# Delta rule on one Trainium2 core: the transposed inverse from a TensorE transpose and a ScalarE copy, in place of a product and a VectorE subtraction

## The chip, the cores and the metric

The kernel runs on one core of a Trainium2 chip. The metric is the device time of one execution, in microseconds; three executions are shown, and the number that counts is their median. Engines are named as the profile names them: PE is TensorE (PEld its weight loads), DVE is VectorE, ACT is ScalarE, POOL is GpSimd, SP is the engine that issues the DMAs.

## The reference

The kernel computes one step of a two-layer backbone over 1024 sample tokens and 256 context tokens. The change touches one part of layer 0, the gated delta rule, which runs in two directions over the tokens with four heads of 128 channels. For each chunk of tokens the reference does

```
decay = jnp.where(tri_incl, jnp.exp(jnp.where(tri_incl, diff, 0.0)), 0.0)
lmat = jnp.where(tri_strict, jnp.einsum('bnhik,bnhjk->bnhij', kb, kc) * decay, 0.0)
amat = lmat + jnp.eye(C, dtype=q.dtype)
sol = lax.linalg.triangular_solve(amat, rhs, left_side=True, lower=True, unit_diagonal=True)
...
def step(s, xs):
    v_new = u_i - jnp.einsum('bhck,bhkv->bhcv', w_i, s)
    o = jnp.einsum('bhck,bhkv->bhcv', qd_i, s) + jnp.einsum('bhij,bhjv->bhiv', qk_i, v_new)
    s = s * cd_i[..., None, None] + jnp.einsum('bhck,bhcv->bhkv', kd_i, v_new)
```

What matters here is the solve with a unit triangular matrix; everything is fp32.

## The kernel before

The program is a list of stages that are written out one behind the other for each engine, with semaphores between the engines. The stage in question is the delta rule in `mixer_even`. It takes the 1280 tokens in chunks of 128 (`IT` is 10 of them) and inverts the 128x128 unit triangular matrix of each head and chunk by doubling. There are seven levels (`LEVELS`). Level 0 gives an inverse of 2x2 blocks, levels 1 to 6 (`LV`) join two blocks of the inverse to one of twice the size. The kernel holds the inverse twice: `Y`, and its transpose `X`. Four heads of 128 columns lie in one bank of 512, so a product of "four heads" is four matmuls of 128x128 in fp32, which the trace shows as eight instructions, and a transpose of four heads is four instructions.

Level `v` consists of two stages, `r` and `u`:

- In stage `r` GpSimd masks the triangular matrix for this level (`lm`, line 1319, into one of two buffers), TensorE multiplies mask and Y (`r`, line 1169, bank 0), and ScalarE copies the product to SBUF as `R` (line 1290).
- In stage `u` TensorE forms R<sup>T</sup>X (`q`, line 1173, bank 1; not at level 6, where nobody needs X any more), and X<sup>T</sup>R (`u`, line 1174, bank 2). VectorE subtracts the first from X (`x`) and the second from Y (`y`), both through the helper at line 1203. The next level's `r` waits for `y`.

Ahead of the levels stand the stages start, decay, rates, exps, scores, mask and inverse, which make the decay factors, the triangular matrix and the first X and Y (X transposed at line 1161, copied at line 1287). Behind them stand state, new and out: KS (line 1180), two VectorE steps, the new values (line 1183, copied by ScalarE at line 1293), the outputs (lines 1189 and 1190) and the state's update (line 1192).

The order is written out by hand: `SCHEDULE` steps through the 22 stages of a chunk for the forward direction (`d` 0) and, `LAG` = 3 stages behind it, the backward direction (`d` 1), and every engine follows that one list. So in the levels TensorE's queue reads: r of forward level k, q and u of backward level k-2, q and u of forward level k, r of backward level k-1, r of forward level k+1. Each direction has four banks of PSUM and buffers of its own. Within the first chunk the list also carries four pieces of pooling work, at the forward stages u1 to u4: an ACT copy (line 1053) and a POOL subtraction (line 1057) each.

Of the kernel before, what the change touches and what calls it, by code (L numbers as in the profile page):

```python
# [41 lines left out]
LEVELS = 7  # L42
# [117 lines left out]
def build(nc, A, OUT):  # L160
    with ExitStack() as ctx:
# [515 lines left out]
        def mixer_even(before_norm, prev, h_ready, early):  # L677
# [399 lines left out]
                ring_out.load(eng, i, w_out[:, :, m * P:(m + 1) * P], (KD, P))  # L1077
            pn = ["gb", "gc", "kk", "qk", "kt", "vt", "xt"]
            for v in LV:
                pn += [f"r{v}"] + ([f"q{v}"] if v < LEVELS - 1 else []) + [f"u{v}"]  # L1080
            pn += ["ks", "vn", "o", "ds"]
            vn = ["gu", "gc", "ta", "tb", "tc", "gl", "l", "qk", "nb", "kd", "vb", "x"]
            for v in LV:
                vn += ([f"x{v}"] if v < LEVELS - 1 else []) + [f"y{v}"]
            vn += ["r1", "r2", "o", "s1", "s2"]
            pe_d = [steps(f"pe_dn{d}", pn, IT) for d in "fb"]
            ve_d = [steps(f"ve_dn{d}", vn, IT) for d in "fb"]
            ac_d = [steps(f"ac_dn{d}", ["eb", "ea", "cd", "eq", "eg", "egl", "y"] + [f"r{v}" for v in LV] + ["vn"], IT) for d in "fb"]
            po_d = [steps(f"po_dn{d}", ["lb", "lm0", "qd"] + [f"lm{v}" for v in LV], IT) for d in "fb"]
            s_state, s_new = sem("state_landed"), sem("state_stored")  # L1090
            s_zb = sem("z_back")
# [41 lines left out]
            @program("pe")  # L1133
            def _(eng):
                ended(eng, *part1, *part2)
                eng.wait_ge(s_small, 64)

                def heads(d, b, f):
                    for hd in range(HEADS):
                        m = f(bank(d, b)[:, hd, :], hd)  # L1140
                    return m
                for stage, d, it in SCHEDULE:
                    pe, ve, ac, po, bf, cs = pe_d[d], ve_d[d], ac_d[d], po_d[d], B[d], cols(it, d)
                    v = int(stage[1:]) if stage[1:].isdigit() else 0
                    if stage == "decay":
                        eng.wait_ge(ve.sem, ve.at("gu", it))
                        if it:
                            eng.wait_ge(ac.sem, ac.at("vn", it - 1))
                        eng.matmul(PS[:, 4 * d, :], ones, bf["R"].rearrange("p h t -> p (h t)"), start=True, stop=True).then_inc(*pe.did("gb", it))
                        eng.matmul(PS[:, 4 * d + 3, 0:4], SQM[:, d, :], GG[:, chunk(it, d), 4 * d:4 * d + 4], start=True, stop=True).then_inc(*pe.did("gc", it))  # L1150
                        heads(d, 1, lambda o, hd: eng.matmul(o, KT[:, hd, cs], KT[:, hd, cs], start=True, stop=True)).then_inc(*pe.did("kk", it))
                        heads(d, 2, lambda o, hd: eng.matmul(o, KT[:, hd, cs], QT[:, hd, cs], start=True, stop=True)).then_inc(*pe.did("qk", it))
                    elif stage == "scores":
                        eng.wait_ge(ve.sem, ve.at("gc", it))
                        heads(d, 3, lambda o, hd: eng.transpose(o, KT[:, hd, cs], ident)).then_inc(*pe.did("kt", it))
                        eng.wait_ge(ve.sem, ve.at("gl", it))
                        eng.wait_ge(ac.sem, ac.at("eq", it))
                        heads(d, 0, lambda o, hd: eng.transpose(o, VT[:, hd, cs], ident)).then_inc(*pe.did("vt", it))
                    elif stage == "inverse":
                        eng.wait_ge(ve.sem, ve.at("x", it))  # L1160
                        heads(d, 3, lambda o, hd: eng.transpose(o, bf["X"][:, hd, :], ident)).then_inc(*pe.did("xt", it))
                    elif v and stage[0] == "r":
                        if v == 1:
                            eng.wait_ge(ac.sem, ac.at("y", it))
                        else:
                            eng.wait_ge(ve.sem, ve.at(f"y{v - 1}", it))
                        eng.wait_ge(po.sem, po.at(f"lm{v}", it))
                        lm = bf[f"M{v % 2}"]
                        heads(d, 0, lambda o, hd: eng.matmul(o, lm[:, hd, :], bf["Y"][:, hd, :], start=True, stop=True)).then_inc(*pe.did(f"r{v}", it))  # L1169
                    elif v:  # L1170
                        eng.wait_ge(ac.sem, ac.at(f"r{v}", it))
                        if v < LEVELS - 1:
                            heads(d, 1, lambda o, hd: eng.matmul(o, bf["R"][:, hd, :], bf["X"][:, hd, :], start=True, stop=True)).then_inc(*pe.did(f"q{v}", it))  # L1173
                        heads(d, 2, lambda o, hd: eng.matmul(o, bf["X"][:, hd, :], bf["R"][:, hd, :], start=True, stop=True)).then_inc(*pe.did(f"u{v}", it))  # L1174
                    elif stage == "state":
                        if it:
                            eng.wait_ge(ve.sem, ve.at("s2", it - 1))
                        else:
                            eng.wait_ge(s_state, 32)
                        heads(d, 3, lambda o, hd: eng.matmul(o, KT[:, hd, cs], bf["S"][:, hd, :], start=True, stop=True)).then_inc(*pe.did("ks", it))  # L1180
                    elif stage == "new":
                        eng.wait_ge(ve.sem, ve.at("r2", it))
                        heads(d, 0, lambda o, hd: eng.matmul(o, bf["Y"][:, hd, :], bf["R"][:, hd, :], start=True, stop=True)).then_inc(*pe.did("vn", it))
                    elif stage == "out":
                        eng.wait_ge(ac.sem, ac.at("vn", it))
                        eng.wait_ge(po.sem, po.at("qd", it))

                        def out(o, hd):
                            eng.matmul(o, bf["S"][:, hd, :], bf["QD"][:, hd, :], start=True, stop=False)  # L1189
                            return eng.matmul(o, bf["VN"][:, hd, :], bf["QK"][:, hd, :], start=False, stop=True)  # L1190
                        heads(d, 1, out).then_inc(*pe.did("o", it))
                        heads(d, 2, lambda o, hd: eng.matmul(o, bf["KD"][:, hd, :], bf["VN"][:, hd, :], start=True, stop=True)).then_inc(*pe.did("ds", it))

            @program("ve")
            def _(eng):
                ended(eng, *part1, *part2)
                eng.wait_ge(s_small, 64)
                for stage, d, it in SCHEDULE:
# [31 lines left out]
                    elif v and stage[0] == "u":  # L1230
# [3 lines left out]
                            eng.wait_ge(ac.sem, ac.at("y", it))  # L1234
                        else:
                            eng.wait_ge(ve.sem, ve.at(f"y{v - 1}", it))
                        if v < LEVELS - 1:
                            tt(f"x{v}", bf["X"], bf["X"], bank(d, 1), ALU.subtract)
                        tt(f"y{v}", bf["Y"], bf["Y"], bank(d, 2), ALU.subtract)
                    elif stage == "state":  # L1240
                        eng.wait_ge(pe.sem, pe.at("ks", it))
# [25 lines left out]
            @program("ac")  # L1267
            def _(eng):
                ended(eng, *part1, *part2)
                for stage, d, it in SCHEDULE:  # L1270
                    pe, ve, ac, bf, cc = pe_d[d], ve_d[d], ac_d[d], B[d], C[d]
                    v = int(stage[1:]) if stage[1:].isdigit() else 0
                    if (d, it) == (0, 0) and stage in POOL_AT_STAGE:
                        pool_hi(eng, POOL_AT_STAGE.index(stage))
                    if (stage, d, it) == ("start", 0, NS // P):
                        ring_out.hi(eng, 0)
                    if stage == "exps":
                        eng.wait_ge(ve.sem, ve.at("gl", it))
                        eng.activation(bf["QK"], bf["QK"], ACT.Exp).then_inc(*ac.did("eb", it))
                        eng.activation(bf["L"], bf["L"], ACT.Exp, scale=-1.0).then_inc(*ac.did("ea", it))  # L1280
                        eng.activation(cc["cd"], bank(d, 0)[:, :, LAST[d]], ACT.Exp).then_inc(*ac.did("cd", it))
                        eng.activation(bf["QD"], bank(d, 0), ACT.Exp).then_inc(*ac.did("eq", it))
                        eng.activation(cc["eg"], cc["gc"], ACT.Exp).then_inc(*ac.did("eg", it))
                        eng.activation(cc["egl"], cc["gl"], ACT.Exp).then_inc(*ac.did("egl", it))
                    elif stage == "inverse":
                        eng.wait_ge(pe.sem, pe.at("xt", it))
                        eng.activation(bf["Y"], bank(d, 3), ACT.Copy).then_inc(*ac.did("y", it))
                    elif v and stage[0] == "r":
                        eng.wait_ge(pe.sem, pe.at(f"r{v}", it))
                        eng.activation(bf["R"], bank(d, 0), ACT.Copy).then_inc(*ac.did(f"r{v}", it))  # L1290
                    elif stage == "new":
                        eng.wait_ge(pe.sem, pe.at("vn", it))
                        eng.activation(bf["VN"], bank(d, 0), ACT.Copy).then_inc(*ac.did("vn", it))
# [1371 lines left out]
```

## Time and profile before

| | |
|---|---|
| median of 3 runs | 4584.02 us (4581.57 to 4584.15) |
| the profiled execution | 4592.9 us, of which its span 4591.1 us |
| busy over the whole span | PE 89%, PEld 75%, DVE 52%, ACT 22%, POOL 25% |
| mean granted TensorE clock | 0.947 |

Times in the trace count from the start of the span. A line of the timeline gives start, length, engine, line of the code, operation, what it writes and reads, how many instructions are merged into it, and in brackets how long the engine was idle before it and who released it. Weight loads (PEld) run ahead of their matmuls; the distance between the starts of two PEld groups is what a group takes of TensorE's time. The clock column is the share of full clock that TensorE was granted: 1.00 is 2.4 GHz and 0.50 is 1.2 GHz.

### The profile page before, as it was taken

To read this page: it belongs to the slowest core of one execution; us is meant where nothing else is said; L and a number is where in the kernel's file an instruction comes from. 1 tells how busy PE (TensorE), PEld (TensorE's weight loads), DVE (VectorE), ACT (ScalarE), POOL (GpSimd) and SP (SyncE) were. 2 spreads that over 40 slices of the span, in tenths; PEclk is the share of its full clock that TensorE was granted. 3 is DMA by queue.
4 is the path that set the end of the run, shared out by engine and by line. 5 is a ranking of instruction groups with operands and counts; after the bars stand their busy time and mean duration, and the time that the engine had idled before them with its cause. 6 is when DMAs were issued, how large, how long until landed. Compare 5 with 4: busy or idle time off the path is not lost.

```text
span 4591.1 us, 52229 instructions
## 1 busy us (share of the span) xinstructions
PE 4094.1 (89%) x22424; PEld 3442.3 (75%) x22424; DVE 2404.3 (52%) x2654; ACT 1031.2 (22%) x1460; POOL 1156.0 (25%) x579
## 2 busy tenths in 40 slices
PE   5899788778989999999969999987667899999998
PEld 3687677777768888888747777776556688888886
DVE  4373445554235444434457556679982445444443
ACT  3153221221131111111233343211111311111112
POOL 1111334333242222222331000022221422222224
PEclk7999999999889999999979999988888899999998
DMA  6511000000212122122122222241321011111111
GB/s 240 164 35 32 29 1 1 1 19 3 85 42 60 56 66 64 59 60 60 42 95 66 85 96 79 72 157 67 122 94 37 23 42 36 36 37 37 41 37 68
DMA packets 309550, 280.99 MB, mean 61 GB/s; under 512 B 8885, under 2 KB 285830, under 8 KB 305831
## 3 DMA queue, kind: packets, MB, share of 16 engines
q1 hardware_dynamic: 309320, 277.65, 18.4%
q8 instruction: 178, 2.92, 0.3%
q14 instruction: 52, 0.43, 0.0%
HBM read 219.94 MB, written 57.67 MB: 60 GB/s over the span
## 4 chain that ended last, share of the span: by engine, by line
PE 64%; DVE 17%; issue 3%; ACT 2%; POOL 2%; DMA 1%; SPq 0%; POOLq 0%; DVEq 0%; ACTq 0%
PE PS L670 47%; DVE piece L1783 8%; PE PS L1851 5%; DVE piece L1203 3%; PE PS L1173 2%; PE PS L1174 2%; PE PS L1169 2%; PE PS L2024 1%; DVE piece L2192 1%; DVE piece L1719 1%; PE PS L1624 1%; ACT piece L510 1%; DVE piece L2220 1%; DVE piece L2195 0%; PE PS L1189 0%
## 5 line engine op out<-in xcount | busy, mean ns | idle before, releaser
L670 PE MATMUL PS<-piece,piece 128*128 128x512 f32 (+1 forms) x13896 | 2810.1, 362 | 79.8 <-POOL piece L545 36.8
L670 PEld LDWEIGHTS PS<-piece,piece 128*128 128x128 f32 x13896 | 2322.5, 191 | 539.5 <-issue 107.0
L653 POOL TENSOR_TENSOR piece<-piece,piece 128x1024 fp32r<-128x1024 f32 (+1 forms) x205 | 507.7, 2477 | 2581.9 <-ACT piece L647 2581.9
L1851 PE MATMUL PS<-piece,piece 128*128 128x256 f32 x1920 | 441.6, 392 | 128.1 <-DVE piece L2478 111.4
L1719 DVE SCALAR_TENSOR_TENSOR piece<-piece,piece,piece 128x1024 f32<-128x1024 f32 x352 | 534.8, 1519 | 12.6
L1851 PEld LDWEIGHTS PS<-piece,piece 128*128 128x128 f32 x1920 | 376.7, 197 | 188.2 <-DVE piece L2478 114.2
L1739 DVE SCALAR_TENSOR_TENSOR piece<-PS,piece,piece 128x1024 f32<-128x1024 f32 x224 | 187.8, 880 | 417.2 <-PE PS L670 417.2
L647 ACT ACTIVATE piece<-piece 128x1024 fp32r<-128x1024 f32 (+1 forms) x205 | 206.4, 1007 | 662.5 <-PE PS L670 615.4
L1203 DVE TENSOR_TENSOR piece<-piece,PS 128x512 f32<-128x512 f32 x288 | 185.4, 684 | 265.3 <-PE PS L1174 206.8
L1716 DVE TENSOR_SCALAR piece<-piece,piece 128x1024 f32<-128x1024 f32 x44 | 35.8, 813 | 514.5 <-ACT piece L1666 514.5
L1169 PE MATMUL PS<-piece,piece 128*128 128x128 f32 x960 | 142.6, 295 | 57.1 <-DVE piece L1203 39.5
L1669 ACT ACTIVATE piece<-piece 128x1280 f32<-128x1280 f32 x44 | 56.1, 1274 | 607.5 <-DVE piece L1727 607.5
L1319 POOL TENSOR_TENSOR piece<-piece,piece 128x512 f32<-128x512 f32 x120 | 159.7, 1345 | 116.0 <-PE PS L1169 116.0
L1783 DVE TENSOR_TENSOR piece<-piece 128x512 f32<-128x512 f32 (+2 forms) x168 | 179.0, 1066 | 17.9 <-ACT piece L2443 11.7
L1169 PEld LDWEIGHTS PS<-piece,piece 128*128 128x128 f32 x960 | 123.4, 201 | 72.9 <-DVE piece L1203 51.9
L1783 DVE SCALAR_TENSOR_TENSOR piece<-piece 128x512 f32<-128x512 f32 (+1 forms) x288 | 163.0, 566 | 9.9
L2192 DVE TENSOR_TENSOR piece<-piece,PS 128x512 f32<-128x512 f32 x80 | 52.9, 684 | 176.9 <-PE PS L2024 176.9
L2457 POOL TENSOR_TENSOR piece<-piece,piece 128x512 f32<-128x512 f32 x40 | 57.5, 1438 | 340.6 <-DVE piece L2478 340.6
L1290 ACT ACTIVATE piece<-PS 128x512 f32<-128x512 f32 x120 | 71.7, 597 | 289.1 <-PE PS L1169 289.1
L1665 ACT ACTIVATE piece<-PS 128x1024 f32<-128x1024 f32 x44 | 45.3, 1029 | 401.4 <-PE PS L670 401.4
L1685 POOL TENSOR_TENSOR piece<-piece,piece 128x1280 fp32r<-128x1280 f32 x44 | 129.9, 2952 | 1.9 <-ACT piece L1673 1.5
L1174 PE MATMUL PS<-piece,piece 128*128 128x128 f32 x960 | 128.3, 280 | 0.0
(238 smaller groups left out, 3505.3 us busy)
## 6 DMA issues: line engine op xcount, KB each, us to landing
piece<-in_l_ffn_up SPq DMA_DIRECT2D x88, 512.0 KB, 3.7
piece<-in_l_w_in SPq DMA_DIRECT2D x45, 512.0 KB, 3.7
piece<-in_l_ada_w SPq DMA_DIRECT2D x44, 512.0 KB, 5.2
piece<-in_l_ada_w SPq DMA_DIRECT2D x18, 1024.0 KB, 7.9
piece<-in_l_ffn_down SPq DMA_DIRECT2D x48, 384.0 KB, 3.0
piece<-filters_s SPq DMA_DIRECT2D x8, 2176.0 KB, 9.6
filters_s<-piece SPq DMA_DIRECT2D x64, 256.0 KB, 2.0
hyena_tokens<-piece SPq DMA_DIRECT2D x24, 640.0 KB, 4.0
```

The source lines that it names most:

```text
L647: eng.activation(HI[i % 2][0][:, 0:n], RAW[i % raws][:, 0:n], ACT.Copy).then_inc(*self.ac.did("hi", i))
L653: eng.tensor_tensor(LO[i % 2][0][:, 0:n], RAW[i % raws][:, 0:n], HI[i % 2][1][:, 0:n], ALU.subtract)\
L670: m = eng.matmul(PS[:, bank + b, 0:n], w, x[:, a:a + n], start=first and n_ == 0, stop=last and n_ == 2)
L1169: heads(d, 0, lambda o, hd: eng.matmul(o, lm[:, hd, :], bf["Y"][:, hd, :], start=True, stop=True)).then_inc(*pe.did(f"r{v}", it))
L1174: heads(d, 2, lambda o, hd: eng.matmul(o, bf["X"][:, hd, :], bf["R"][:, hd, :], start=True, stop=True)).then_inc(*pe.did(f"u{v}", it))
L1203: eng.tensor_tensor(out, a, b, op).then_inc(*ve.did(step, it))
L1319: eng.tensor_tensor(bf[f"M{v % 2}"], bf["L"], over(LVM[:, d, v, :], HEADS), ALU.mult).then_inc(*po.did(f"lm{v}", it))
L1685: eng.tensor_tensor(hl, CV[j % 2], hh, ALU.subtract).then_inc(*po.did("lo", j))
L1719: eng.scalar_tensor_tensor(acc, src, w, acc, ALU.mult, ALU.add).then_inc(*ve.did(f"grid{k}", j))
L1739: eng.scalar_tensor_tensor(XT[:, mm, a:a + n], PSF[:, at_:at_ + n], MOD[:, layer, 40 + mm, c:c + 1], XT[:, mm, a:a + n], ALU.mult, ALU.add ...
L1783: f(*args).then_inc(*st.did(f"{tag}{n[0]}", rnd))
L1851: m = eng.matmul(PS[:, bank, o * HC:(o + 1) * HC], M[i][o], rhs[i], start=i == 0, stop=i == 1)
```

## The change

At levels 2 to 6 X is no longer updated by a product and a subtraction. Once Y of the level before is there, TensorE transposes it into bank 1 (`t`, right behind `r` in its queue), and ScalarE copies that bank to X (`x`, right behind the copy of R in its queue). Stage u waits for this copy, which stands behind that of R. At level 1 X is still what the stage before the levels left, so there is neither a product nor a transpose. Level 6, which had no update of X, now has a transpose and a copy like the others.

```
-                pn += [f"r{v}"] + ([f"q{v}"] if v < LEVELS - 1 else []) + [f"u{v}"]
+                pn += [f"r{v}"] + ([f"t{v}"] if v > 1 else []) + [f"u{v}"]
...
                         heads(d, 0, lambda o, hd: eng.matmul(o, lm[:, hd, :], bf["Y"][:, hd, :], start=True, stop=True)).then_inc(*pe.did(f"r{v}", it))
+                        if v > 1:
+                            heads(d, 1, lambda o, hd: eng.transpose(o, bf["Y"][:, hd, :], ident)).then_inc(*pe.did(f"t{v}", it))
...
-                        eng.wait_ge(ac.sem, ac.at(f"r{v}", it))
-                        if v < LEVELS - 1:
-                            heads(d, 1, lambda o, hd: eng.matmul(o, bf["R"][:, hd, :], bf["X"][:, hd, :], start=True, stop=True)).then_inc(*pe.did(f"q{v}", it))
+                        eng.wait_ge(ac.sem, ac.at(f"r{v}" if v == 1 else f"x{v}", it))
                         heads(d, 2, lambda o, hd: eng.matmul(o, bf["X"][:, hd, :], bf["R"][:, hd, :], start=True, stop=True)).then_inc(*pe.did(f"u{v}", it))
...
-                        if v < LEVELS - 1:
-                            tt(f"x{v}", bf["X"], bf["X"], bank(d, 1), ALU.subtract)
                         tt(f"y{v}", bf["Y"], bf["Y"], bank(d, 2), ALU.subtract)
...
                         eng.activation(bf["R"], bank(d, 0), ACT.Copy).then_inc(*ac.did(f"r{v}", it))
+                        if v > 1:
+                            eng.wait_ge(pe.sem, pe.at(f"t{v}", it))
+                            eng.activation(bf["X"], bank(d, 1), ACT.Copy).then_inc(*ac.did(f"x{v}", it))
```

## Rows read from the trace of the kernel before

**Rows 1.** the page's chain that ended last, share of the span by line

```profile
PE PS L670 47%; DVE piece L1783 8%; PE PS L1851 5%; DVE piece L1203 3%; PE PS L1173 2%; PE PS L1174 2%; PE PS L1169 2%; PE PS L2024 1%; DVE piece L2192 1%; DVE piece L1719 1%; PE PS L1624 1%; ACT piece L510 1%; DVE piece L2220 1%; DVE piece L2195 0%; PE PS L1189 0%
```

**Rows 2.** groups of instructions, 473 to 1152 us: count, busy us, mean ns, idle before

```profile
L1203 DVE TENSOR_TENSOR piece<-piece,PS 128x512 f32<-128x512 f32 x288 | 185.4, 684 | 265.3 <-PE PS L1174 206.8 <-PE PS L1192 43.8 <-ACT piece L1280 14.1
L1319 POOL TENSOR_TENSOR piece<-piece,piece 128x512 f32<-128x512 f32 x120 | 159.7, 1345 | 116.0 <-PE PS L1169 116.0
L1169 PE MATMUL PS<-piece,piece 128*128 128x128 f32 x960 | 142.6, 295 | 57.1 <-DVE piece L1203 39.5 <-POOL piece L1319 10.6 <-ACT piece L1287 6.9
...
L1173 PE MATMUL PS<-piece,piece 128*128 128x128 f32 x800 | 112.8, 287 | 0.0
...
L1057 POOL TENSOR_TENSOR piece<-piece,piece 128x1280 fp32r<-128x1280 f32 x4 | 11.6, 2895 | 11.2 <-ACT piece L1053 11.2
```

**Rows 3.** the timeline, one level of both directions: start us, us, engine, line

```profile
906.63 1.16 PE L1169 MATMUL PS<-piece,piece 128*128 128x128 f32 x8 [0.48 <-DVE piece L1203]
...
907.83 0.60 ACT L1290 ACTIVATE piece<-PS 128x512 f32<-128x512 f32 x1 [1.04 <-PE PS L1169]
...
908.41 0.97 PEld L1174 LDWEIGHTS PS<-piece,piece 128*128 128x128 f32 x8
...
909.30 0.97 PEld L1173 LDWEIGHTS PS<-piece,piece 128*128 128x128 f32 x8
...
909.61 1.28 DVE L1203 TENSOR_TENSOR piece<-piece,PS 128x512 f32<-128x512 f32 x2 [3.04 <-PE PS L1174]
...
911.09 0.97 PEld L1169 LDWEIGHTS PS<-piece,piece 128*128 128x128 f32 x8
...
911.40 1.28 DVE L1203 TENSOR_TENSOR piece<-piece,PS 128x512 f32<-128x512 f32 x2 [0.50 <-PE PS L1174]
...
912.74 1.16 PE L1169 MATMUL PS<-piece,piece 128*128 128x128 f32 x8 [0.48 <-DVE piece L1203]
```

**Rows 4.** the timeline, two groups of four transposes, one behind the other

```profile
949.08 0.47 PEld L1155 LDWEIGHTS PS<-piece,piece 128*128 128x128 f32 x4
...
949.52 0.47 PEld L1158 LDWEIGHTS PS<-piece,piece 128*128 128x128 f32 x4
```

**Rows 5.** the timeline of GpSimd, the mask of level 2

```profile
898.44 1.27 POOL L1319 TENSOR_TENSOR piece<-piece,piece 128x512 f32<-128x512 f32 x1
```

**Rows 6.** the timeline, level 2's and level 6's first product and the end

```profile
900.06 1.16 PE L1169 MATMUL PS<-piece,piece 128*128 128x128 f32 x8 [1.38 <-DVE piece L1203]
...
924.96 1.16 PE L1169 MATMUL PS<-piece,piece 128*128 128x128 f32 x8 [0.48 <-DVE piece L1203]
...
935.44 0.30 PEld L1189 LDWEIGHTS PS<-piece,piece 128*128 128x128 f32 x2
...
938.12 0.97 PEld L1174 LDWEIGHTS PS<-piece,piece 128*128 128x128 f32 x8
```

**Rows 7.** the timeline of ScalarE, Y of the forward direction in four chunks

```profile
892.50 0.60 ACT L1287 ACTIVATE piece<-PS 128x512 f32<-128x512 f32 x1 [9.46 <-PE PS L1161]
...
957.58 0.60 ACT L1287 ACTIVATE piece<-PS 128x512 f32<-128x512 f32 x1 [9.45 <-PE PS L1161]
...
1023.90 0.60 ACT L1287 ACTIVATE piece<-PS 128x512 f32<-128x512 f32 x1 [9.28 <-PE PS L1161]
...
1091.06 0.60 ACT L1287 ACTIVATE piece<-PS 128x512 f32<-128x512 f32 x1 [9.46 <-PE PS L1161]
```

**Rows 8.** the chain in order of time, at half clock: transposes, and a product

```profile
895.23 0.85 PE PS L1155 x4
...
968.65 1.71 PE PS L1173 x8
```

**Rows 9.** the last transposes: timeline, then clock in stretches of them (PE, PEld, PEclk)

```profile
4574.70 9.11 PE L2563 MATMUL PS<-piece,piece 128*128 128x128 f32 x56 [1.40 <-DVE piece L2575]
...
4574.70:4578.70 4.00, 4.00 (x19) 4.00 (x20) 0.50 0.45 178
...
4579.70:4583.80 4.10, 3.97 (x34) 3.41 (x32) 1.00 0.95 385
```

More of the change, by code:

```diff
@@ L1083, in mixer_even @@
             for v in LV:
-                vn += ([f"x{v}"] if v < LEVELS - 1 else []) + [f"y{v}"]
+                vn += [f"y{v}"]
             vn += ["r1", "r2", "o", "s1", "s2"]
@@ L1087, in mixer_even @@
             ve_d = [steps(f"ve_dn{d}", vn, IT) for d in "fb"]
-            ac_d = [steps(f"ac_dn{d}", ["eb", "ea", "cd", "eq", "eg", "egl", "y"] + [f"r{v}" for v in LV] + ["vn"], IT) for d in "fb"]
+            ac_d = [steps(f"ac_dn{d}", ["eb", "ea", "cd", "eq", "eg", "egl", "y"] + [f"{t}{v}" for v in LV for t in "rx" if t == "r" or v > 1] + ["vn"], IT) for d in "fb"]
             po_d = [steps(f"po_dn{d}", ["lb", "lm0", "qd"] + [f"lm{v}" for v in LV], IT) for d in "fb"]
```

## The prediction

> **What bounds the kernel now.** I read the page's chain first, for the share of the span that the change can touch. The big products at line 670 hold 47% of it; the delta rule appears as VectorE's line 1203 with 3% and TensorE's lines 1173, 1174 and 1169 with 2% each [rows 1]. It is a serial stage on the path that ends last, so what it saves comes off the total. The groups of instructions in that stage come next. Line 1173, the product that the change takes out, has 800 instructions, 100 groups of eight; line 1169 waited for VectorE 39.5 us, for GpSimd 10.6 us and for ScalarE 6.9 us [rows 2]. TensorE and VectorE alternate here, and GpSimd's masks are late only rarely.
>
> The timeline then shows one level of both directions (F forward, B backward). F's r starts at 906.63, its next one at 912.74 [rows 3]: 6.11 us. A group of four heads takes 0.89 us of TensorE (908.41 to 909.30). In its queue stand r of F, q and u of B, q and u of F, r of B: six groups, 5.34 us, and a gap of 0.77. The loop closes through F alone: F's u ends at 911.09, VectorE starts 0.31 us later, needs 1.28 us for x and y, and r starts 0.06 us after that [rows 3]. Two things thus set the period: six groups, and a VectorE turn that only B's r covers in part.
>
> **Part 1: q goes, t comes.** 100 products of 0.89 us leave TensorE. 100 transposes of four heads come; two such groups stand back to back at 949.08 and 949.52 [rows 4], so 0.44 us each. TensorE saves 45 us of work. These are fp32 transposes of four 128x128 tiles as well, so the row is the price and needs no bounds.
>
> **Part 2: VectorE's x goes.** Each turn shrinks from 1.28 to 0.68 us [rows 2, 3].
>
> **Part 3: ScalarE's copy comes, and u waits for it.** The copy of R starts 1.20 us after r's first instruction and lasts 0.60 (907.83 against 906.63) [rows 3]. The transposes end 1.33 us after r's start and could be copied from 1.64, 0.31 later, so R is last, not t. The copy of X comes behind R: from 1.80 to 2.40, and u may start at 2.46 with the hand-over of 0.06. For the copy I take 0.60, the same shape out of the same kind of bank. From below, a copy that overlapped R's until the transposes allow it would end at 2.24; from above, twice a copy, 1.20, would end it at 3.00. Behind the waiting u on TensorE stands r of the other direction; behind the waiting copy on ScalarE stands the other direction's copy of R. Both are in the sums below. No DMA is issued, and SP waits for nothing new.
>
> **Part 4: the new period.** Count from F's r. r to 0.89, t to 1.33, u of B to 2.22 (its X was copied in the half-turn before), wait to 2.46, u of F to 3.35, r of B to 4.24, t of B to 4.68. F's y: 3.35 plus 0.31 plus 0.68 plus 0.06 is 4.40, so F's next r starts at 4.68. B's y is ready at 3.27, before r of B is wanted at 3.35. TensorE now sets the period but for a wait of 0.24: 4.68 in place of 6.11, 1.43 less.
>
> **Part 5: one interval** (F's and B's chunk side by side).
> - Level 1 to 2: the first u comes 0.89 earlier and VectorE's turn is shorter, which would put F's r of level 2 at about 898.6. The mask of level 2 ends at 899.71 [rows 5]; the r starts then in place of 900.06 [rows 6]. Saved 0.33, and GpSimd is what is late next.
> - Level 2 to 3: before, 6.57 us (900.06 to 906.63). After: R from 1.20, X copied to 2.40, u from 2.46 to 3.35, y and hand-over 1.05: 4.40. Saved 2.17. The transpose of B's first X in between is 1.2 us earlier too, since VectorE comes to it earlier by the first x and the first q.
> - Levels 3 to 6: three periods, 4.29.
> - From F's r of level 6 (924.96) to B's u of level 6 (938.12) [rows 6]: 13.16 us before. After: eight groups (r, u, r, KS, u, new values, r of B, u of B's level 5 among them) 7.12, three transposes 1.32, the outputs 2.68 (935.44 to 938.12 [rows 6]), and the waits: 0.24 for each of two X copies, and 0.62 for VectorE's two steps behind KS, so far covered by B's q and u. Sum 12.22, saved 0.94. Here level 6 pays for a transpose and a copy that it did not have.
>
> The sum is 7.7 us. What follows, from state to the next chunk's first Y, has neither step and shifts as it is.
>
> **Part 6: ten intervals.** The four starts of Y shown lie 65.08, 66.32 and 67.16 us apart [rows 7]; of the eight regular intervals five have 65.08. The longer ones have the half clock in a bad place: a group of products costs 1.71 and of transposes 0.85 there [rows 8]. The first interval is another case: four GpSimd pieces of 2.9 us, each waiting for a ScalarE copy that follows a copy of R [rows 2], make masks late (the 10.6 us). The new X copy stands ahead of three of them and adds some 0.6 us each, which takes nearly all that its last levels gain: I count zero. Nine times 7.7 is **69 us**.
>
> The profiled execution (4592.9 us) would become 4524; it is 8.9 us above the median of 4584.02. On the median the sum gives 4515 us.
>
> **Rivals.**
> 1. *The half clock falls among the levels.* The stretch at half clock, about one per interval, lies now mostly beside work that other engines bound; with another interval length it may land in levels that TensorE itself sets. The three long intervals paid 1.2 to 2.1 us for it. At 2 us in each of nine: 18 us given back, 4533. For it: TensorE has little slack left in the new period. Against: five of eight pay nothing.
> 2. *The X copy is slow to be handed over.* If it takes the upper bound, u starts at 3.06 and the period is 5.28: 0.60 lost in each of six turns per interval, 32 us over nine, 4547. The copies of R in the trace speak against it: 0.60 each [rows 3].
> 3. *The masks become the bound, no gain.* GpSimd needs two masks a period, 2.7 us at their mean of 1345 ns [rows 2]; it would need 3.05 each to hold the period at 6.11. 4584 then; only the first interval looks like that.
> 4. *Slower: transposes let the clock fall.* If TensorE ran at half clock through the levels, the period would be four groups of 1.71 and two transposes of 0.85, 8.54 in place of 6.11: 7.3 us lost over three periods. The end would take 8 x 1.71 + 3 x 0.85 + 2 x 2.68 = 21.6 in place of 13.2, 8.4 lost, and level 2 about 1. That is 17 us an interval, 150 over nine: 4734 us. It decides from the point where a third of the levels' time runs so: 7.7 gained against 24.4 (17 and 7.7) lost. Against it stand the kernel's last 56 transposes, a TensorE stretch of nothing else: it began at 0.50 and reached 1.00, which it held from 4579.70 on [rows 9]. The Trainium skill, in "TensorE: Matmul & The Clock Gate", section "Part 4: PE-mode transpose", says that transposes don't count as busy and leave the clock at its lower level; by it this rival would be the likely one. The trace disagrees with the rule in that stretch, so I give it little.
>
> **How the numbers follow.** The forecast, 4515, gets 0.78; rival 1, 0.10; rival 2, 0.06; rival 3, 0.02; rival 4, 0.04. The range starts at 4500: with the lower bound of the copy TensorE's 4.44 us sets the period, a further 0.24 less in each of six turns, about 9.1 us saved per interval, 82; the rest of the way to 4500 is the excess of the long intervals, if it goes. It ends at 4547 with the slow copy, and so holds about nine in ten. A measurement of this kernel tells some 0.2% (9 us) from no change: faster 0.94, same 0.02, slower 0.04.
>
> **What would show it.** In the changed trace F's r of one level should follow that of the level before by 4.6 to 4.7 us; line 1173 should be gone and 400 instructions of transposes be there at 0.44 a group; ScalarE should copy twice back to back, the second ending 2.4 us after r's start; VectorE should have one subtraction a turn; intervals should be near 57.4 us, the first near 78. I am wrong if the X copy ends later than 3.0, if GpSimd releases r within the levels of later chunks, or if the clock column shows 0.50 through levels 3 to 6.

## The result, and the profile after

The changed kernel takes 4520.4 us (median of 4 runs, 4517.9 to 4522.6) against 4584.09 us (4581.57 to 4587.15) beside it: ratio 0.9854 [0.9843, 0.9865], 63.7 us saved. The forecast was 4515, its range 4500 to 4547.

The profiled execution (4520.36 us, span 4518.5 us) has this chain that ended last, from the page:

```profile
PE PS L670 47%; DVE piece L1784 8%; PE PS L1852 5%; PE PS L1169 2%; DVE piece L1203 2%; PE PS L1174 2%; PE PS L2025 1%; PE PS L1171 1%; DMA piece<-hyena_tokens 1%; DVE piece L2193 1%; DVE piece L1720 1%; POOL piece L1311 1%; PE PS L1625 1%;
```

Beside [rows 1], VectorE's line 1203 has 2% in place of 3%; the product of line 1173 (2%) is gone and the transposes, now line 1171, have 1%. The groups of instructions of the delta rule, 473 to 1090 us, answer to [rows 2] (the masks are line 1320 now, the R copy 1288, the X copy 1291):

```profile
L1320 POOL TENSOR_TENSOR piece<-piece,piece 128x512 f32<-128x512 f32 x120 | 158.0, 1337 | 56.3 <-PE PS L1169 55.9
L1169 PE MATMUL PS<-piece,piece 128*128 128x128 f32 x960 | 142.5, 297 | 43.2 <-POOL piece L1320 36.3 <-ACT piece L1285 6.9
...
L1203 DVE TENSOR_TENSOR piece<-piece,PS 128x512 f32<-128x512 f32 x188 | 126.5, 686 | 250.8 <-PE PS L1174 189.7 <-PE PS L1192 46.3 <-ACT piece L1278 14.1
...
L1171 PE MATMUL PS<-piece,piece 128*128 128x128 f32 x400 | 64.2, 286 | 0.0
L1291 ACT ACTIVATE piece<-PS 128x512 f32<-128x512 f32 x100 | 59.2, 592 | 2.3 <-PE PS L1171 2.3
```

Three things are to be seen. The 288 subtractions are 188. Line 1169 no longer waits for VectorE (39.5 us before) but for GpSimd's masks: 36.3 us where 10.6 stood, 18.2 of it in the first interval and 18.2 behind it. And the X copies waited 2.3 us in all for the transposes, so they stand right behind the R copies. One level of both directions, from the timeline (columns as in [rows 3]):

```profile
755.93 0.97 PEld L1169 LDWEIGHTS PS<-piece,piece 128*128 128x128 f32 x8
...
756.82 0.47 PEld L1171 LDWEIGHTS PS<-piece,piece 128*128 128x128 f32 x4
...
757.13 0.60 ACT L1288 ACTIVATE piece<-PS 128x512 f32<-128x512 f32 x1 [0.24 <-PE PS L1169]
757.26 1.98 PEld L1174 LDWEIGHTS PS<-piece,piece 128*128 128x128 f32 x16
...
757.63 0.59 ACT L1291 ACTIVATE piece<-PS 128x512 f32<-128x512 f32 x1
758.46 0.69 DVE L1203 TENSOR_TENSOR piece<-piece,PS 128x512 f32<-128x512 f32 x1 [2.91 <-PE PS L1174]
759.21 0.97 PEld L1169 LDWEIGHTS PS<-piece,piece 128*128 128x128 f32 x8
...
760.53 0.97 PEld L1169 LDWEIGHTS PS<-piece,piece 128*128 128x128 f32 x8
```

F's r comes again after 4.60 us (6.11 before). The R copy starts 1.20 after r, as before; the X copy starts 0.50 behind it, not 0.60, and ends at 758.22, 2.29 after r's start. The u of B and of F are merged into one block of 16 there. Cut at 758.24, the timeline of TensorE's loads shows where the eight loads of F's u begin:

```profile
758.27 0.97 PEld L1174 LDWEIGHTS PS<-piece,piece 128*128 128x128 f32 x8
```

The u of B begins at 757.26 and takes 0.89, so TensorE could go on at 758.15. F's u waits 0.12 more and begins 0.05 behind the end of the X copy (758.22). It ends at 759.16, and r of B begins at 759.21, 0.06 behind the end of B's subtraction (758.46 and 0.69). The same two small waits stand in all 36 such blocks behind the first chunk. The chain in order of time (start, us, what) holds nothing but TensorE there:

```profile
756.20 0.89 PE PS L1169 x8
757.10 0.44 PE PS L1171 x4
757.53 1.90 PE PS L1174 x16
759.43 0.94 PE PS L1169 x8
760.37 0.44 PE PS L1171 x4
760.80 0.89 PE PS L1169 x8
```

0.89 + 0.44 + 1.90 + 0.94 + 0.44 is 4.61: TensorE's queue is the whole period. Its work is 4.44 of that (four groups of 0.89, two of 0.44); the rest is the two waits, which the chain counts into u (1.90) and r (0.94). What closes the loop is u of B (0.89), B's subtraction with its hand-overs (1.05), then r and t of B and r and t of F (2.66): 4.60. The u of F runs beside that subtraction, and its wait for the X copy is nearly covered by it.

**Where the 63.7 us came from.** The unchanged kernel was run again with a profile (below: "before again"), because the profile of before was a long execution, and the changed one too ("after again"). The intervals between the first X transposes of F (line 1161) in consecutive chunks, the last one up to the store of the final state, in us:

| | first | the eight regular ones | last |
|---|---|---|---|
| before | 77.84 | 66.66, five of 65.08, 66.32, 67.15 | 61.82 |
| before again | 77.72 | 66.70, five of 65.07 or 65.08, 64.71, 65.08 | 61.93 |
| after | 79.93 | three of 57.01, five of 57.82 to 58.19 | 52.23 |
| after again | 81.97 | 56.99 and 57.00, six of 57.87 to 58.29 | 52.23 |

Against "before again" the stage shrank by 67.7 us (661.50 to 593.77): 60.2 in the regular intervals and 9.7 in the last, less 2.2 that the first one lost. Between before and "after again" it shrank by 68.1 (665.19 to 597.09). What lies behind the stage took 3436.3 us in "before again" and 3437.8 in after; over all fourteen profiles it lies between 3432.6 and 3443.2, though no edit touches it.

### The profile page after: what moved, and what is told of

Same layout as the page of the kernel before. It is cut to its first block, busy times and chain, and to the rows that moved or that the text cites. A ratio compares the mean times of both kernels' runs of the same rounds, so it can differ in the third digit from the quotient of the medians.

```text
span 4518.5 us, 51429 instructions
## 1 busy us (share of the span) xinstructions
PE 4047.1 (90%) x22024; PEld 3400.1 (75%) x22024; DVE 2342.4 (52%) x2554; ACT 1080.9 (24%) x1560; POOL 1155.1 (26%) x579
## 4 chain that ended last, share of the span: by engine, by line
PE 64%; DVE 16%; POOL 3%; issue 2%; ACT 2%; DMA 2%; SPq 0%; POOLq 0%; DVEq 0%; ACTq 0%
PE PS L670 47%; DVE piece L1784 8%; PE PS L1852 5%; PE PS L1169 2%; DVE piece L1203 2%; PE PS L1174 2%; PE PS L2025 1%; PE PS L1171 1%; DMA piece<-hyena_tokens 1%; DVE piece L2193 1%; DVE piece L1720 1%; POOL piece L1311 1%; PE PS L1625 1%; DVE piece L2221 1%; ACT piece L510 0%
## 5 line engine op out<-in xcount | busy, mean ns | idle before, releaser
L1203 DVE TENSOR_TENSOR piece<-piece,PS 128x512 f32<-128x512 f32 x188 | 126.5, 686 | 250.8 <-PE PS L1174 189.7
L1169 PE MATMUL PS<-piece,piece 128*128 128x128 f32 x960 | 142.5, 297 | 43.2 <-POOL piece L1320 36.3
L2193 DVE TENSOR_TENSOR piece<-piece,PS 128x512 f32<-128x512 f32 x80 | 52.8, 684 | 175.3 <-PE PS L2025 175.3
L2444 ACT ACTIVATE piece<-PS 128x512 f32<-128x512 f32 x80 | 47.8, 597 | 350.0 <-PE PS L1852 350.0
```

The lines of the kernel that those rows point to most:

```text
L1203: eng.tensor_tensor(out, a, b, op).then_inc(*ve.did(step, it))
```

## The experiments

Each kernel was timed against the unchanged kernel on the same chip. "Period" is F's r to F's next r within the levels; "stage" runs from the first X transpose to the store of the final state.

**Both kernels again.** No edit.

> The kernel before once more, with a profile of its own. Its profiled execution had been 4592.9 us and its runs 4581.6 to 4587.2, so the changed kernel gained 72 us in the traces and 64 us in the medians. Theory A (the stretches at half clock fall differently in each execution): the regular intervals are 65.08 us again where no half clock falls among the levels, the delta rule ends up to 8 us earlier, and the rest of the span is the same to 1 or 2 us. Theory B (the difference lies elsewhere in the kernel): the delta rule takes 677 us again and the rest differs.

Measured: 4585.9 us, ratio 1.0002 [0.9993, 1.0011]. Its profiled execution took 4580.36 us, where that of before took 4592.9; the first X transpose stands at 480.79 against 486.99, and the stage took 661.50 against 665.19. So 6.2 us of before's excess lay ahead of the stage, where the change touches nothing, 3.7 in it and 2.6 behind it. Neither theory had that: the half clock within the stage can account for the 3.7 at most.

> The changed kernel once more, with a profile of its own. Theory A: its regular intervals are 57.0 us where no half clock falls among the levels and about 58.2 where one does, the first 79.9; the ratio to the kernel before is 0.985 again (0.984 to 0.987).

Measured: 4520.0 us, 0.9852 [0.9832, 0.9872]. The regular intervals are as expected, 57.0 twice and 57.87 to 58.29 six times; the first is not: 81.97 in place of 79.9.

**What all of X costs.** The transposes and the X copy go, and u waits for R alone.

```diff
-                        if v > 1:
-                            heads(d, 1, lambda o, hd: eng.transpose(o, bf["Y"][:, hd, :], ident)).then_inc(*pe.did(f"t{v}", it))
...
-                        eng.wait_ge(ac.sem, ac.at(f"r{v}" if v == 1 else f"x{v}", it))
+                        eng.wait_ge(ac.sem, ac.at(f"r{v}", it))
...
-                            eng.activation(bf["X"], bank(d, 1), ACT.Copy).then_inc(*ac.did(f"x{v}", it))
```

> Levels 2 to 6 keep the X of level 0: no transposes, no copies of X. Part of the computation is left out. Theory A (the chain r, copy of R, copy of X, u, y sets the period, with TensorE close behind): the period falls from 4.60 to 3.80 us, an interval from 57.0 to 52.9, the kernel from 4520 to about 4480 us. Theory B (TensorE's work alone decides and the copy is hidden): 0.44 us less for each of 100 transposes, 44 us spread over two directions, the period falls by 0.88 to 3.7 and the time to 4476; the two differ here by little, and the next run separates them.

Measured: 4480.6 us, 0.9775 [0.976, 0.9789]; period 3.78, as Theory A had it (3.80, where B had 3.7), stage 556.2; the times of the two theories lie too near to be told apart. So, with all else as it is, 39.8 us is the most that a still faster way to X could give: the change took 63.7 of 103.5.

**The X copy twice.** ScalarE copies the bank once more, ahead of the real copy, into a buffer that is free then.

```diff
+                            eng.activation(bf["VN"], bank(d, 1), ACT.Copy).then_inc(*ac.did(f"w{v}", it))
                             eng.activation(bf["X"], bank(d, 1), ACT.Copy).then_inc(*ac.did(f"x{v}", it))
```

> ScalarE copies the transposed bank twice, first to a buffer that nobody reads, then to X. Theory A (the copy stands on the chain): 0.5 us more per turn, the period 5.1, an interval 60, the kernel 4520 plus 29, 4549 us. Theory B (the copy is hidden beside TensorE's work): no change, 4520.

Measured: 4543.4 us, 0.9918 [0.9902, 0.9935]. The chain in order of time over one period:

```profile
762.78 0.60 ACT piece L1288
763.38 0.49 ACT piece L1291
763.87 0.49 ACT piece L1292
764.36 0.49 ACT piece L1288
764.85 0.49 ACT piece L1291
765.34 0.50 ACT piece L1292
765.83 0.04 issue
765.88 1.16 PE PS L1174 x8
767.04 0.91 PE PS L1169 x8
767.94 0.02 issue
767.97 0.60 ACT piece L1288
```

The period is 5.19, and it closes through ScalarE: six copies of 0.49 to 0.60, then u and r. Take the two extra copies (0.98) out and the same loop is 4.21, below the 4.60 of TensorE. So in the changed kernel ScalarE's queue has 0.4 us a period to spare, and does not set the period; the X copy holds up only u of F, by the 0.12 that B's subtraction nearly covers. The expectation came out in size (period 5.1, 4549 us), the mechanism as the rows tell it: it is ScalarE's whole queue that counts, not the one late copy.

**The X copy on VectorE.**

```diff
-                            eng.activation(bf["X"], bank(d, 1), ACT.Copy).then_inc(*ac.did(f"x{v}", it))
...
+                        eng.tensor_copy(bf["X"], bank(d, 1)).then_inc(*ve.did(f"x{v}", it))
```

> VectorE copies the transposed bank to X, in place of ScalarE, at the same stage. Theory A: VectorE has room there (the copy would run from 1.64 to 2.32 us after r starts, the other direction's y from 2.53), so the period stays near 4.60 and the kernel at 4520, at most 2 us less in the first interval; that ScalarE does it is not where the gain comes from. Rival (VectorE's turn was the bound, and any second operation on it costs its 0.6 us again): 0.6 us per turn, 60 us over 100 turns less what overlaps, 4560 to 4580.

Measured: 4517.4 us, 0.9855 [0.984, 0.9869]; period 4.66, with two VectorE operations a turn as in the kernel before (6.11). That it is ScalarE that copies gives nothing: what helps is that the subtraction no longer stands behind u on the path.

**The transpose as a product with the identity.** Same bank, same order, but eight instructions of a product in place of four of a transpose.

```diff
-                            heads(d, 1, lambda o, hd: eng.transpose(o, bf["Y"][:, hd, :], ident)).then_inc(*pe.did(f"t{v}", it))
+                            heads(d, 1, lambda o, hd: eng.matmul(o, bf["Y"][:, hd, :], ident, start=True, stop=True)).then_inc(*pe.did(f"t{v}", it))
```

> Each transpose is replaced by a product of Y with the unit matrix, which gives the same X at a product's price (0.89 us for four heads in place of 0.44). Theory A (TensorE's six groups and the chain set the period): the period rises from 4.60 to about 5.4, an interval from 57.0 to 61.3, the kernel to about 4559 us; most of what the change gains over the period of 6.11 then remains with the removed VectorE step and the order. Rival (transposes let the clock fall, products hold it): the clock column shows fewer stretches at 0.50 than in the changed kernel, and the time comes out below 4545.

Measured: 4564.6 us, 0.9957 [0.994, 0.9974]. One period, from the table of stretches (PE busy, PEld, DVE, ACT, POOL, clock, DMA share, GB/s):

```profile
843.72:849.24 5.52, 5.52 (x51) 5.50 (x50) 1.38 (x2) 2.39 (x4) 1.28 (x2) 1.00 0.01 3
```

The period rises by 0.92, about twice the 0.45 by which a product exceeds a transpose, since TensorE is busy throughout. Of the 63.7 us, 44.2 hang on the transpose being half as long as a product; the other 19.5 are what is gained even at a product's price, with the subtraction off the path and a copy beside TensorE's work in its place. One sign of the rival did appear: over the eight regular intervals the granted clock is 0.98, where the changed kernel had 0.96 (0.95 in "after again"). Its time, below 4545, did not. And the transposes are not what sets that clock: over the same intervals it is 0.95 in the run without any in the levels ("What all of X costs"), and 0.98 in the next run, which has all of them.

**Transposes ahead of r.** t and the X copy go ahead of r and the R copy; u waits for R.

```diff
+                        if v > 1:
+                            heads(d, 1, lambda o, hd: eng.transpose(o, bf["Y"][:, hd, :], ident)).then_inc(*pe.did(f"t{v}", it))
                         eng.wait_ge(po.sem, po.at(f"lm{v}", it))
...
                         heads(d, 0, lambda o, hd: eng.matmul(o, lm[:, hd, :], bf["Y"][:, hd, :], start=True, stop=True)).then_inc(*pe.did(f"r{v}", it))
-                        if v > 1:
-                            heads(d, 1, lambda o, hd: eng.transpose(o, bf["Y"][:, hd, :], ident)).then_inc(*pe.did(f"t{v}", it))
```

> The transposes stand ahead of r in TensorE's queue and the copy of X ahead of that of R. Theory A: u then waits for the copy of R, 2.30 us after the turn's start, the period is 4.5 in place of 4.6; at level 2 the transposes run while r waits for its mask, 0.44 less. About 0.9 us per interval, 8 us in all, and 2 us in the first interval: 4510 us. Rival (the copy of X hides behind TensorE anyway): 4520, no change.

Measured: 4499.5 us, 0.9813 [0.9799, 0.9828], 20.9 us under the changed kernel, where Theory A had 10. The period fell little, 4.60 to 4.55; regular intervals went from 57.01 to 56.43. The timeline at F's level 2 shows one place:

```profile
739.14 0.42 PEld L1168 LDWEIGHTS PS<-piece,piece 128*128 128x128 f32 x4 [0.97 <-DVE piece L1203]
...
740.40 0.97 PEld L1171 LDWEIGHTS PS<-piece,piece 128*128 128x128 f32 x8 [0.83 <-POOL piece L1320]
```

The transposes now run while r still waits for the mask. Seven of eight regular intervals lie at 56.43 to 56.59, so the long ones are nearly gone, and the last interval took 48.8. The stage shrank by 13.2 (593.8 to 580.5); the remaining 7.7 of the 20.9 us lie outside it in the two profiles, where the edit does nothing. Behind the stage it is 5.2 (3437.8 to 3432.6), and there the clock records of the traces hold 342 us at half clock in after and 327 here; why the half clock falls less often there stays open.

**Masks one level early.** GpSimd makes the mask of level v+1 at stage r of level v, so that no r waits for it.

```diff
-                        eng.tensor_tensor(bf[f"M{v % 2}"], bf["L"], over(LVM[:, d, v, :], HEADS), ALU.mult).then_inc(*po.did(f"lm{v}", it))
+                        for lv in ((1, 2) if v == 1 else (v + 1,) if v + 1 < LEVELS else ()):
...
+                            eng.tensor_tensor(bf[f"M{lv % 2}"], bf["L"], over(LVM[:, d, lv, :], HEADS), ALU.mult).then_inc(*po.did(f"lm{lv}", it))
```

> GpSimd makes each mask from level 2 on one stage earlier, in time that it spends waiting. Theory A (at level 2 the mask is what is late next, and in the first interval the masks are late behind the pooling pieces): about 1.2 us less in each of nine intervals, 8 us in the first, 4501 us; no idle time of line 1169 put down to GpSimd after the first interval. Rival (at level 2 the next thing, VectorE's x of the other direction, is late at once): 4515 to 4520.

Measured: 4506.6 us, 0.9829 [0.9815, 0.9844], between the two theories; but the gain is the first interval's alone (79.93 to 66.77), and no regular one is under 57.52, where after has three of 57.01. F's r of level 2 did start 1.94 behind u of level 1 rather than 3.25, and line 1169 waited for GpSimd 7.8 us in place of 36.3. But 7.8 us of waiting for VectorE came instead, and u of level 1 itself stands 1.09 later in its interval. The timeline of after, one interval's beginning (GpSimd and VectorE):

```profile
738.42 1.72 POOL L1320 TENSOR_TENSOR piece<-piece,piece 128x512 f32<-128x512 f32 x1
...
739.85 1.45 DVE L1203 TENSOR_TENSOR piece<-piece,piece 128x512 f32<-128x512 f32 x2
```

and the same place with the early masks, with the ScalarE step that waits:

```profile
838.77 3.41 POOL L1321 TENSOR_TENSOR piece<-piece,piece 128x512 f32<-128x512 f32 x2
...
840.20 2.52 DVE L1203 TENSOR_TENSOR piece<-piece,piece 128x512 f32<-128x512 f32 x2
...
842.83 0.63 ACT L1277 ACTIVATE piece<-piece 128x512 f32<-128x512 f32 x1 [2.12 <-DVE piece L1203]
```

The second mask of GpSimd runs beside two VectorE operations that read both inputs from SBUF: they take 2.52 in place of 1.45, and B's exponentials, which were idle 1.04 there, wait 2.12. That is the 1.07 us that B's whole chunk starts later. B's first r then comes 0.84 later, and F's r of level 3, behind it in TensorE's queue, 0.68.

**The pooling pieces ahead of the chunks.** The four GpSimd pieces move from the levels u1 to u4 of the first chunk to its early stages.

```diff
-            POOL_AT_STAGE = ["u1", "u2", "u3", "u4"]
+            POOL_AT_STAGE = ["start", "decay", "rates", "exps"]
```

> The four pooling pieces (a copy on ScalarE and a subtraction on GpSimd each) move from the first chunk's stages u1 to u4 to its stages start to exps. Theory A (they make the first interval 79.9 us in place of 57.0, since GpSimd's masks stand behind them and each waits for a copy that now follows the copy of X): the first interval falls to about 63 us, with the first masks 5 us later, the kernel to 4503. Rival (the first interval is long for other reasons, cold queues or the half clock): 4515 to 4520.

Measured: 4507.5 us, 0.9829 [0.9813, 0.9846]. The first interval is 58.03, like any other (63 expected), but it starts at 497.33, 10.4 later than in after (5 expected): the four pieces stand ahead of the first masks, and behind the DMA that brings the masks' constants. From the timeline of GpSimd:

```profile
481.75 11.43 POOL L1057 TENSOR_TENSOR piece<-piece,piece 128x1280 fp32r<-128x1280 f32 x4 [31.39 <-DMA piece<-in_k_level]
```

**Both, and the pieces split.** Transposes first, two pieces at the start and two behind the levels.

```diff
-            POOL_AT_STAGE = ["u1", "u2", "u3", "u4"]
+            POOL_AT_STAGE = ["start", "decay", "state", "state"]
```

> Transposes first, as in the run before, and the pooling pieces at places where ScalarE and GpSimd wait: two at the first chunk's stages start and decay (GpSimd idles until its first mask there), two at its stage state. Theory A (the pieces ahead of the masks are all that makes the first interval long): its start doesn't move, and it falls from 78.6 to between 57 and 60 us; the kernel from 4499.5 to about 4480 us. Rival (the pieces only move the wait, as when all four stood ahead and the first Y came 10.4 us later): 4488 or more.

Measured: 4495.1 us, 0.9809 [0.9793, 0.9825], the rival's side. The first interval fell from 78.56 to 63.70, the stage from 580.5 to 565.3, yet the time by 4.4 only, inside the scatter of the two. 3.4 us are the later start (487.87 against 484.44: the two pieces stand there behind the masks' DMA); what lies behind the stage took 7.0 us more in this profile (3439.6 against 3432.6), with 351 us at half clock in the clock records against 327. Why the half clock falls so there stays open.

**The best version, and one more try.** On top of that, GpSimd's product for the outputs (`qd`) goes behind the last mask, and F's mask of level 2 is made ahead of B's `lb`.

```diff
+                        if d == 1:
...
+                            eng.wait_ge(ve.sem, ve.at("gl", it))
+                            eng.tensor_tensor(B[0]["M0"], B[0]["L"], over(LVM[:, 0, 2, :], HEADS), ALU.mult).then_inc(*po_d[0].did("lm2", it))
...
+                        if v == LEVELS - 1:
...
+                            eng.tensor_tensor(bf["QD"], bf["QD"], QT[:, :, cols(it, d)], ALU.mult).then_inc(*po.did("qd", it))
```

> In addition the forward direction's mask of level 2 is made before the backward direction's first mask, when VectorE has just ended its SBUF work, and the product for QD on GpSimd goes from the stage inverse to behind the last mask. Theory A (at level 2 GpSimd's mask is late by 1.3 us; the run with all masks early gave it back because VectorE's two SBUF operations beside a GpSimd operation took 2.52 in place of 1.45 us, and because the backward direction's first mask stood behind QD): 1.2 us less in each of nine intervals, 4468 to 4471 us. Rival (contention moves to another pair of operations): intervals of 56.4 us as before, 4480.

Measured: 4486.9 us, 0.9783 [0.9768, 0.9797], 33.5 us under the changed kernel; regular intervals 55.26, 1.17 less as expected, the first one still 63.81. The time missed its 4468 to 4471: that was reckoned from the 4480 expected of the run before, which took 4495.1. From there the gain is 8.2 us, where nine times 1.2 would be 10.8. The groups of instructions of the stage show that the masks are hardly late any more (20.2 us with the transposes ahead of r alone):

```profile
L1171 PE MATMUL PS<-piece,piece 128*128 128x128 f32 x960 | 131.3, 281 | 12.1 <-ACT piece L1287 6.9 <-POOL piece L1325 5.2
```

The last kernel moves the two early pieces ahead of GpSimd's wait for the mask constants as well (and the fourth piece to the stage out).

```diff
+                for g in range(2):
+                    pool_lo(eng, g)
                 eng.wait_ge(s_mask, 16)
```

> As the run before, but the first two pooling pieces don't stand behind GpSimd's wait for the mask constants (they had waited until 478 us for that DMA and put off the first Y by 4.5 us), and the last one goes behind the backward direction's last mask, which had waited 5.45 us for two pieces. Theory A: the first Y 4 us earlier, the first interval 63.8 less 3, the kernel 4480 to 4483 us. Rival (the last piece now puts off the first chunk's output, which waits for all pieces, by as much): 4484 to 4487.

Measured: 4488.6 us, 0.9784 [0.9767, 0.98]. The first interval is 60.64, but there is no gain that can be measured. The time is on the rival's side; the rival's reason is not shown, since the profiled executions lie at opposite ends here (4480.2, the shortest of five, against 4494.9, the longest of five in the run before).

## Why the prediction was right, and where its terms were off

- **Part 1** held: 400 transpose instructions, 0.44 us a group. The product with the identity shows that TensorE's time was the larger part of the gain (44.2 of 63.7).
- **Part 2** held: 188 subtractions at 686 ns, one a turn.
- **Part 3** was a little too dear. I put the X copy behind the end of the R copy, from 1.80 to 2.40. It starts 0.50 behind R's start and ends at 2.29, so u of F starts at 2.34 and not at 2.46. The Trainium skill, in "ScalarE: Activation LUTs", section "What ACT_TABLE_LOAD costs", says that consecutive activations overlap by about 93 ns; the trace agrees (757.13 to 757.63 for a copy of 0.60).
- **Part 4**: period 4.60, not 4.68. The wait for the X copy is 0.12, not 0.24, and behind it r of B waits 0.05 for B's subtraction, which is ready at 3.27 (759.21 against 755.93), just where Part 4 had it. From there r and t of B take 1.33, and 4.60 is the period. So TensorE's queue does bound it, as said, but the lower end of the range was reckoned wrongly: with a faster copy TensorE's 4.44 could not have set the period, since Part 4's own 3.27 and 1.33 leave it at 4.60. A faster copy had 0.08 a period to give, not 0.24.
- **Part 5**: for the interval that starts at 739.07 the four terms came out at 0.25, 3.82, 3.02 and 0.99 (forecast 0.33, 2.17 + 1.43, 2.86 and 0.94): 8.08 for 7.7. They are read from F's r at 740.41, 747.07, 755.93 and 765.13 and u of B at 777.30, against 893.15, 900.06, 912.74, 924.96 and 938.12. Of the step named next late, the trace shows just that, the mask of level 2 ending at 746.95 and r behind it:

```profile
745.69 1.26 POOL L1320 TENSOR_TENSOR piece<-piece,piece 128x512 f32<-128x512 f32 x1
...
747.10 1.13 PE L1169 MATMUL PS<-piece,piece 128*128 128x128 f32 x8 [2.12 <-POOL piece L1320]
```

- **Part 6, the first interval**, is the term that I had on the wrong side: counted zero, it cost 2.2 (4.3 in "after again"). I priced the copy ahead of each pooling copy, but not that GpSimd, waiting for it, is also late with the next mask. GpSimd was idle 14.4 us ahead of three of its pieces (11.2 before [rows 2]), and TensorE then waited for the masks:

```profile
503.87 2.88 POOL L1057 TENSOR_TENSOR piece<-piece,piece 128x1280 fp32r<-128x1280 f32 x1 [4.54 <-ACT piece L1053]
...
518.11 2.04 PE L1169 MATMUL PS<-piece,piece 128*128 128x128 f32 x8 [4.27 <-POOL piece L1320]
```

- **Rival 1** came true in part, and is the other reason for 4520 and not 4515. Two consecutive intervals of the changed kernel in the table of stretches, the first of 57.01 us (741.00 to 751.00, and one period of its levels), the second of 58.19 (798.08 to 808.08), at the same places but for 0.07:

```profile
core 0: us, PE busy (x) PEld busy (x) DVE busy (x) ACT busy (x) POOL busy (x), PEclk, DMA share, GB/s
741.00:744.40 3.40, 2.17 (x19) 1.76 (x18) 1.65 (x4) 2.37 (x7) 1.04 (x1) 1.00 0.00 0
747.00:751.00 4.00, 3.60 (x30) 3.39 (x31) 0.98 (x2) 1.57 (x3) 4.00 (x3) 1.00 0.02 4
...
755.93:760.53 4.60, 4.60 (x42) 4.57 (x41) 1.38 (x2) 2.17 (x5) 2.70 (x4) 1.00 0.00 0
...
798.08:801.48 3.40, 3.26 (x18) 2.89 (x18) 1.57 (x4) 2.38 (x7) 1.05 (x2) 0.55 0.00 0
804.08:808.08 4.00, 3.97 (x20) 3.77 (x21) 1.69 (x3) 1.77 (x3) 4.00 (x3) 0.57 0.01 4
```

  In the second, the stretches of level 1 and then of level 2 ran nearly all at 1.2 GHz (0.55 and 0.57); the work and the waits ahead of them were the same in both. It costs 1.18, and it struck five of eight intervals (57.82 is one of them: its counterpart in before again, 64.71, is 0.36 short of its neighbours): 5.9 us, of which the forecast's arithmetic, made from 65.08, held none. "After again" paid for it in six intervals, "before again" in one. It is far from the 18 us of the rival.
- **Rival 2** did not occur (X copy at 2.29, not 3.00), and was priced too dear. The run with the X copy twice has a period 0.59 longer, and it cost 23.0 us, where the rival had 32 for 0.60: a regular interval grew by 2.69 (57.01 to 59.70), which is four and a half such turns and not six.
- **Rival 3**: masks do set one r in an interval and the first interval, not the period. GpSimd releasing r in later chunks was named as a sign of being wrong, and it came: 18.2 us behind the first interval, in nine waits, all at F's level 2, where Part 5 had put it. The sign was drawn too wide.
- **Rival 4** is refuted: transposes stand in every period, and the clock is 1.00 through the period with two groups of them (755.93 to 760.53 above), as it is in the kernel with products in their place. Over whole intervals the transposes don't set it either: it is 0.95 without them, 0.98 with all of them ahead of r. The rule of the Trainium skill in "TensorE: Matmul & The Clock Gate", "Part 4: PE-mode transpose", did not decide here.
- **The sum.** Eight regular intervals times 8.07 is 64.6; the last gives 9.7, the first takes 2.2; the half clock takes 5.9 where before again lost 1.6: 67.8, against 67.7 measured for the stage. The forecast had 69 from nine equal terms: larger terms (8.07 and 9.7 where it had 7.7) and the losses that it did not have nearly cancel. The mechanism was right; that the sum came within 2 us of the stage is in part luck. The median's 63.7 lies 4 below the stage's 67.7, by what scatters outside the stage from one execution to the next (6 us ahead of it in the two profiles of before, 5 behind it in the two of after).

## What to carry to other kernels

Where two engines alternate on a serial loop, write down the queue of each engine over one period, and each loop that goes through two engines, and add them up. The longest sum is the period, here the loop through B's subtraction (4.60); what lies a few tenths under it (TensorE's own work, 4.44, and the loop through ScalarE's copies, 4.21) is the next bound. A merged block in a timeline can hide a wait; look at its loads one by one before calling an engine full. A transpose that replaces a product of the same tiles pays twice: it is half as long, and what follows it is a copy that ScalarE or VectorE can make in the same kernel time (4520.4 and 4517.4 us). When a loop shrinks, look at once at those who delivered to it with slack before; here it was GpSimd's masks, which went from 10.6 to 36.3 us of waiting, and making them early gave 1.17 us in each regular interval once the mask no longer ran beside VectorE's pair of SBUF operations (1.30 us there in the best version, 2.52 before); until then it gave nothing there.

## What the runs showed of the hardware that was not expected

VectorE and GpSimd slow each other when VectorE reads two operands from SBUF. A VectorE operation on two SBUF tiles of 128x512 took 1.73 us beside a GpSimd operation of 1.27 that had started before it; without GpSimd at work beside it, none of 88 in this stretch of the kernel took more than 0.69. One with an input from PSUM kept its 0.69 beside GpSimd. Where the VectorE operation started first it kept 0.68, and the GpSimd operation took 1.80. From the timeline of after, VectorE and GpSimd:

```profile
737.20 1.27 POOL L1314 TENSOR_TENSOR piece<-piece,piece 128x512 f32<-128x512 f32 x1
737.28 1.73 DVE L1203 TENSOR_TENSOR piece<-piece,piece 128x512 f32<-128x512 f32 x1 [0.17 <-POOL piece L1311]
...
739.12 0.69 DVE L1203 TENSOR_TENSOR piece<-PS,piece 128x512 f32<-128x512 f32 x1
...
746.89 0.68 DVE L1203 TENSOR_TENSOR piece<-piece,piece 128x512 f32<-128x512 f32 x1
746.91 1.80 POOL L1314 TENSOR_TENSOR piece<-piece,piece 128x512 f32<-128x512 f32 x1
```

The Trainium skill, in "SBUF — State Buffer", section "SBUF: two separate sides", says that the two engines share one pair of ports as an exclusive lock, taken by a VectorE operation with two SBUF inputs or by a GpSimd operation, and that the loser waits until it is free. The rows agree in the main: the VectorE operation ends at 739.01, 0.54 behind the GpSimd one that started first, and GpSimd's next (738.42) is stretched to 1.72.
